# Dummy products in TensorE's waits, and feed-forward weights that meet both parts of the tokens in 512 columns

## The reference

```python
# first block, for i in 0, 1
h = x * (1 + sc_m) + sh_m
y = conformer_conv(h, ...) if i == 0 else short_gated_conv(h, ...)
x = layer_norm(ALPHA * x + (1 + g_m) * y, ...)
h = x * (1 + sc_f) + sh_f
y = hierarchical_moe(h, ...)                 # router, 32 experts, 2 of them per token
x = layer_norm(ALPHA * x + (1 + g_f) * y, ...)

# second block, for l in 0, 1
x = layer_norm_2(DN_ALPHA * x + 0.5 * swiglu(x, ffn1_in[l], ffn1_out[l]), ...)
x = layer_norm_2(DN_ALPHA * x + hybrid_mixer(x, ...), ...)
x = layer_norm_2(DN_ALPHA * x + 0.5 * swiglu(x, ffn2_in[l], ffn2_out[l]), ...)

def swiglu(x, w_in, w_out):                  # w_in 1024 x 5632, w_out 2816 x 1024
    gate, up = jnp.split(x @ w_in, 2, axis=-1)
    return (jax.nn.silu(gate) * up) @ w_out
```

## Time and profile before

| | |
|---|---|
| median of 3 runs | 2619.37 us (2616.03 to 2624.01) |
| profiled execution, its own time | 2622.48 us |
| span in its trace | 2620.7 us |
| PE busy | 2448.5 us (93%) |
| PEld busy | 1816.9 us (69%) |
| DVE busy | 1279.0 us (49%) |
| ACT busy | 886.8 us (34%) |
| POOL busy | 304.6 us (12%) |
| mean granted TensorE clock | 0.979 of full |

### The profile page before, as it was taken

How to read it: one execution, slowest core, us unless ns; L and a number is a source line. 1 busy time by engine, 2 the same in 40 slices (tenths; PEclk the granted TensorE clock), 3 DMA queues, 4 the chain that set the end, 5 groups by cost and what they waited for, 6 DMA issues and landing times.

```text
span 2620.7 us, 39277 instructions
## 1 busy us (share of the span) xinstructions
PE 2448.5 (93%) x16044; PEld 1816.9 (69%) x16045; DVE 1279.0 (49%) x2232; ACT 886.8 (34%) x1528; POOL 304.6 (12%) x371
## 2 busy tenths in 40 slices
PE   7999988998898998998899999999999999999998
PEld 4664434443685433343499899889989989988997
DVE  6573323222665332322354586665455458666545
ACT  2341111111332211111144465454444446545443
POOL 0210100000000010000000123330010012333001
PEclk8989999999998999999899999999999999999999
DMA  9987999999783999999937453343743745334371
GB/s 395 370 336 316 420 419 420 419 420 420 273 335 129 419 419 419 419 420 420 390 131 256 158 179 133 128 156 130 256 161 122 264 158 177 127 137 155 129 257 49
DMA packets 246345, 710.56 MB, mean 271 GB/s; under 512 B 11795, under 2 KB 165139, under 8 KB 189587
## 3 DMA queue, kind: packets, MB, share of 16 engines
q1 hardware_dynamic: 243810, 704.94, 70.5%
q10 hardware_dynamic: 2352, 3.06, 0.3%
HBM read 705.46 MB, written 1.05 MB: 270 GB/s over the span
## 4 chain that ended last, share of the span: by engine, by line
PE 72%; DMA 16%; DVE 6%; issue 2%; ACT 2%; POOL 1%; SPq 0%; DVEq 0%; ACTq 0%; POOLq 0%
PE w L899 19%; DMA ring<-in_e_w_up_dram 15%; PE w L1161 11%; PE y L939 11%; PE w L901 9%; PE w L1180 5%; PE w L1420 2%; PE y L1213 2%; PE y L806 1%; PE w L1405 1%; PE w L1135 1%; PE y L1369 1%; PE w L1001 1%; DVE wsp L1525 1%; DMA ring<-in_ada_w_dram 1%
## 5 line engine op out<-in xcount | busy, mean ns | idle before, releaser
L1525 DVE TENSOR_TENSOR wsp<-ring,wsp 128x1024 fp32r<-128x1024 f32 (+1 forms) x464 | 573.1, 1241 | 387.1 <-ACT wsp L1515 386.7
L899 PE MATMUL w<-hh,wsp 128*128 128x256 f32 x4672 | 613.4, 284 | 5.7 <-DVE wsp L1525 4.1
L899 PEld LDWEIGHTS w<-hh,wsp 128*128 128x128 f32 x4672 | 584.7, 191 | 28.5 <-issue 17.3
L1515 ACT CAST wsp<-ring 128x1024 fp32r<-128x1024 f32 (+1 forms) x464 | 482.1, 1045 | 354.4 <-PE w L901 171.9
L1161 PE MATMUL w<-ring,arena 128*64 128x512 f32 x2016 | 459.3, 600 | 77.2 <-DMA ring<-in_e_w_up_dram 72.5
L1161 PEld LDWEIGHTS w<-ring,arena 128*64 128x64 f32 x2016 | 153.8, 137 | 344.2 <-issue 342.3
L901 PE MATMUL w<-hl,wsp 128*128 128x256 f32 x2336 | 327.7, 283 | 0.0
L901 PEld LDWEIGHTS w<-hl,wsp 128*128 128x128 f32 x2336 | 301.3, 192 | 0.0
L939 PE MATMUL y<-wsp,zsp 128*128 128x512 f32 x1104 | 266.8, 391 | 2.9 <-POOL zsp L2747 2.6
L2011 DVE TENSOR_TENSOR ht<-w,ht 128x256 f32<-128x256 f32 x64 | 39.5, 618 | 440.9 <-ACT ht L2543 440.9
L2543 ACT ACTIVATE ht<-w 128x256 f32<-128x256 f32 x64 | 40.0, 626 | 625.3 <-PE w L1161 625.3
(11 more groups left out here) (334 smaller groups left out, 2478.7 us busy)
## 6 DMA issues: line engine op xcount, KB each, us to landing
ring<-in_e_w_gate_dram SPq DMA_DIRECT2D x126, 1024.0 KB, 13.6
ring<-in_e_w_up_dram SPq DMA_DIRECT2D x126, 1024.0 KB, 15.8
ring<-in_e_w_down_dram SPq DMA_DIRECT2D x124, 1024.0 KB, 13.6
ring<-in_ffn_in_dram SPq DMA_DIRECT2D x88, 1024.0 KB, 6.1
ring<-in_ada_w_dram SPq DMA_DIRECT2D x48, 1024.0 KB, 14.6
ring<-in_w_in_dram SPq DMA_DIRECT2D x48, 1024.0 KB, 5.0
ring<-in_ffn_out_dram SPq DMA_DIRECT2D x44, 1024.0 KB, 6.3
ring<-in_b_w_in_dram SPq DMA_DIRECT2D x12, 1024.0 KB, 11.8
```

Source lines behind the costliest of these rows:

```text
L899: pe.matmul(dst, a[:, kc * m:(kc + 1) * m], hh[:, kc, :], start=kc == 0 and j == 0, stop=False)
L1515: ac.copy(shaped(halves(i)[0], u.shape), u.cut(ring[:, u.piece % NSLOT, :])).then_inc(*mark("w_high", i))
L1525: ve.tensor_tensor(shaped(lo, u.shape), u.cut(ring[:, u.piece % NSLOT, :]), shaped(hi, u.shape).bitcast(F32), ALU.subtract).then_inc(*mark ...
```

## The change

Two things are changed. First, a helper `keep_busy(bank, times)` issues float32 products of the identity with 256 columns of `vecs` into a PSUM bank whose content nobody reads. It is called ahead of some waits of TensorE: 4 times in each router before the second token part; 7 times (3 in layer 0) before and after the ranks; 7 times before the last `combine` of each layer; 5 times before part 0 of the norms `ffn0` and `ffn1`; 6 times before part 1 of the norms `n00`, `n01`, `n02`, `n10`, `n11`.

Second, in the feed-forwards the tiles `hh` and `hl` become halves of one tile `hx`. Each high weight piece now meets both at once in one matmul of 512 columns, which puts the two partial sums side by side into a whole bank; the low weight piece adds to the first half. Gate and up therefore take a bank each, and VectorE adds the halves of each with a `tensor_reduce`, the gate into `hid` and the up into `upb`. Silu and the multiplication then read these.

```diff
+            def keep_busy(bank, times):
+                for _ in range(times):
+                    pe.matmul(bank[:, 0:T], ident, vecs[:, 0:T], start=True, stop=True)

             router(l, n):            # for t in range(2):
+                    if t:
+                        keep_busy(WB[2], 4)
             to_feature_later(n):     # for t in range(2):
+                    if n[0:3] == "ffn" and t == 0:
+                        keep_busy(WB[3], 5)
+                    elif n[0] == "n" and t == 1:
+                        keep_busy(WB[0], 6)
                     pe.wait_ge(*at("diag", n, t))
             moe(l, n):
+                keep_busy(WB[0], 7 if l else 3)
                 pe.wait_ge(*at("route_v", l, "oo", 1))
...
+                keep_busy(WB[0], 7 if l else 3)
             combine(p):
+                    pe.wait_ge(*at("ct", l, p))
+                    if p == E // 2 - 1:
+                        keep_busy(WB[moe_banks(l).index(("turn", E - 1)) % 4], 7)
                     pe.wait_ge(*at("ye", "low", l, p))

+            def proj_wide(dst, i):
+                wh, wl = halves(i)
+                pe.wait_ge(*low_done(i))
+                for kc in range(KC):
+                    if kc == KC - 1:
+                        pe.matmul(dst[:, 0:T], wl[:, kc * P:(kc + 1) * P], hh[:, kc, :], start=False, stop=False)
+                    ins = pe.matmul(dst[:, :], wh[:, kc * P:(kc + 1) * P], hx[:, :, kc, :], start=kc == 0, stop=kc == KC - 1)
+                    if kc < KC - 1:
+                        pe.matmul(dst[:, 0:T], wl[:, kc * P:(kc + 1) * P], hh[:, kc, :], start=False, stop=False)
+                ins.then_inc(*mark("w_used", i))

             # TensorE, ffn
-                    b = WB[k % 4]
+                    gate_b, up_b = ffn_banks(k)      # (WB[0], WB[3]) or (WB[1], WB[2])
                     if k == 0:
-                        first_two([b[:, 0:T], WB[3][:, T:2 * T]], i, n)
+                        first_wide([gate_b, up_b], i, n)     # the same 48 matmuls of 256 columns
                     else:
-                        if k >= 3:
-                            pe.wait_ge(*at("hid", key, max(k - 4, 0)))
-                        proj(b[:, 0:T], i)
-                        proj(b[:, T:2 * T], i + 1)
+                        if k >= 2:
+                            pe.wait_ge(*at("up_sum", key, k - 2))
+                        proj_wide(gate_b, i)
+                        proj_wide(up_b, i + 1)

             # VectorE, ffn
+                    weight_lows(ve, i + (2 if k == 0 else 3))
+                    ve.wait_ge(*at("w_used", i))
+                    if k >= 4:
+                        ve.wait_ge(*at("z_lo", key, k - 4))
+                    ve.tensor_reduce(hid[:, k % 4, :], gate_b[:, :].rearrange("p (a t) -> p t a", a=2), AX, ALU.add)
                     weight_lows(ve, i + 4)
+                    ve.wait_ge(*at("w_used", i + 1))
+                    ve.tensor_reduce(upb[:, k % 2, :], up_b[:, :].rearrange("p (a t) -> p t a", a=2), AX, ALU.add)
                     ve.wait_ge(*at("silu_f", key, k))
-                    ve.tensor_tensor(hid[:, k % 4, :], WB[k % 4 if k else 3][:, T:2 * T], hid[:, k % 4, :], ALU.mult)
+                    ve.tensor_tensor(hid[:, k % 4, :], upb[:, k % 2, :], hid[:, k % 4, :], ALU.mult)

             # ScalarE, ffn
-                    ac.wait_ge(*at("w_used", i + 1))
-                    ac.activation(hid[:, k % 4, :], WB[k % 4][:, 0:T], ACT.Silu)
+                    ac.wait_ge(*at("gate_sum", key, k))
+                    ac.activation(hid[:, k % 4, :], hid[:, k % 4, :], ACT.Silu)
```

More of the change, by code:

```diff
@@ L304, in program @@
         vv = sb("vv", [P, 2, D])
-        hh = sb("hh", [P, KC, T], F32R)
-        hl = sb("hl", [P, KC, T], F32R)
+        hx = sb("hx", [P, 2, KC, T], F32R)
+        hh, hl = hx[:, 0, :, :], hx[:, 1, :, :]
         ht = sb("ht", [P, 4, 2, T])
@@ L367, in program @@
         hid = area(0, 4, T)
+        upb = ht[:, 1, :, :]
         vh = zsp[:, :, :, :].rearrange("p a b t -> p (a b t)").rearrange("p (t d) -> p t d", t=2)
@@ L674, in bank_end, with ffn_banks @@
             return f | (1 if t and n != "ffn0" else 3)
+        def ffn_banks(k):
+            return (WB[1], WB[2]) if k % 2 else (WB[0], WB[3])
         def z_tiles(key, f):
@@ L933, in first_two, with first_wide @@
                     ins.then_inc(*mark("w_used", i + u))
+            def first_wide(dsts, i, n):
+                parts = [halves(i + u) for u in range(2)]
+                for u in range(2):
+                    pe.wait_ge(*at("w_high", i + u))
+                    for kc in range(KC):
+                        if u == 0:
+                            pe.wait_ge(*at("h_hi", n, 1, kc))
+                        pe.matmul(dsts[u][:, 0:T], parts[u][0][:, kc * P:(kc + 1) * P], hh[:, kc, :], start=kc == 0, stop=False)
+                for u in range(2):
+                    pe.wait_ge(*low_done(i + u))
+                    for kc in range(KC):
+                        pe.matmul(dsts[u][:, 0:T], parts[u][1][:, kc * P:(kc + 1) * P], hh[:, kc, :], start=False, stop=kc == KC - 1)
+                for u in range(2):
+                    for kc in range(KC):
+                        if u == 0:
+                            pe.wait_ge(*at("h_lo", n, kc, 1))
+                        ins = pe.matmul(dsts[u][:, T:2 * T], parts[u][0][:, kc * P:(kc + 1) * P], hl[:, kc, :], start=kc == 0, stop=kc == KC - 1)
+                    ins.then_inc(*mark("w_used", i + u))
+            def proj_wide(dst, i):
+                wh, wl = halves(i)
+                pe.wait_ge(*low_done(i))
+                for kc in range(KC):
+                    if kc == KC - 1:
[4 more added lines that the diff above has]
+                ins.then_inc(*mark("w_used", i))
             def row_half(k, n, i, zh, zl, t, h):
@@ L1207, in combine @@
                     i = p % 2
+                    pe.wait_ge(*at("ct", l, p))
+                    if p == E // 2 - 1:
+                        keep_busy(WB[moe_banks(l).index(("turn", E - 1)) % 4], 7)
                     pe.wait_ge(*at("ye", "low", l, p))
-                    pe.wait_ge(*at("ct", l, p))
                     for t in range(2):
@@ L2127, in ffn @@
                 for k in range(22):
+                    gate_b, up_b = ffn_banks(k)
+                    weight_lows(ve, i + (2 if k == 0 else 3))
+                    ve.wait_ge(*at("w_used", i))
+                    if k >= 4:
+                        ve.wait_ge(*at("z_lo", key, k - 4))
+                    ve.tensor_reduce(hid[:, k % 4, :], gate_b[:, :].rearrange("p (a t) -> p t a", a=2), AX, ALU.add).then_inc(*mark("gate_sum", key, k))
                     weight_lows(ve, i + 4)
+                    ve.wait_ge(*at("w_used", i + 1))
+                    ve.tensor_reduce(upb[:, k % 2, :], up_b[:, :].rearrange("p (a t) -> p t a", a=2), AX, ALU.add).then_inc(*mark("up_sum", key, k))
+                    ve.wait_ge(*at("up_sum", key, k))
                     ve.wait_ge(*at("silu_f", key, k))
-                    ve.tensor_tensor(hid[:, k % 4, :], WB[k % 4 if k else 3][:, T:2 * T], hid[:, k % 4, :], ALU.mult).then_inc(
+                    ve.tensor_tensor(hid[:, k % 4, :], upb[:, k % 2, :], hid[:, k % 4, :], ALU.mult).then_inc(
                         *mark("hid", key, k))
@@ L2586, in ffn @@
                     weight_highs(ac, i + 4)
-                    if k >= 4:
-                        ac.wait_ge(*at("z_lo", key, k - 4))
-                    ac.wait_ge(*at("w_used", i + 1))
-                    ac.activation(hid[:, k % 4, :], WB[k % 4][:, 0:T], ACT.Silu).then_inc(*mark("silu_f", key, k))
+                    ac.wait_ge(*at("gate_sum", key, k))
+                    ac.activation(hid[:, k % 4, :], hid[:, k % 4, :], ACT.Silu).then_inc(*mark("silu_f", key, k))
                     if k >= 4:
```

## The result

The changed kernel takes 2607.29 us (median of 7 runs, 2604.74 to 2608.85). The kernel before took 2619.37 in the same session (7 runs, 2614.44 to 2625.24). The ratio is 0.995, 95% interval 0.9939 to 0.9961, so it is faster by 12.1 us. The forecast was 20.2 us less, at 2599: right in direction, inside the ends that its terms gave (2592 to 2613), and too large by two thirds. The span in the trace went from 2620.7 to 2605.5, 15.2 us less, and the mean granted clock from 0.979 to 0.991.

What follows compares the result with a forecast made beforehand. TensorE was taken to bound the feed-forwards; -14.5 + 5.4 + 1.2 - 8.0 - 4.5 - 1.7 + 1.9 = -20.2 us gave 2599 us against the median, range 2592 to 2613.

Steps and rivals of the forecast that it cites:

- wide products: Feed-forward projections: merging 8 pairs of matmuls saves 0.086 us in each of 168 projections, 14.5 us off TensorE.
- start of each feed-forward: Block 1's gate product starts some 1.4 us late, as VectorE's subtraction stands behind the reduce of gate 0; +5.4 us.
- ends: End of each feed-forward: a reduce and a subtraction now precede the last z; 0.3 us each, +1.2 in all.
- norms: Norms n00 to n11: six dummies fit TensorE's 3.08 us idle before part 1 and keep the clock up; -8.0 us.
- last combinings: Last combinings and their norms: dummies fit in the waits and the work behind runs at full clock; -4.5 us.
- router, layer 1: Layer 1's router: dummies fill the waits, so ranks and gathering come at full clock; -1.7 us (-3.4 to +1).
- router, layer 0: Layer 0's router: no wait before part 1, so four dummies delay the turn by 1.86 us; +1.9 in sum.
- rival 3: Feed-forwards: VectorE becomes the bound from a reduce of about 2.0 us; about 2645 us at 2.5; chance 0.03.
- rival 2: Norms, combinings, layer 1's router: dummies do not hold the clock, their 14.2 us go; about 2616 us; chance 0.09.
- Rival 4: Projections: a 256-column matmul's extra 13 ns belongs mostly to its columns; merging gains a quarter; about 2610 us; chance 0.03.

Runs made afterwards that it cites:

- experiment 3: The changed kernel with VectorE's subtraction for weight unit 2 back ahead of the reduce of gate 0; 2597.89 us, 0.9914 of the kernel before.
- experiment 1: The kernel before with all the change's dummy products and its own narrow projections; 2609.2 us, 0.9955 of the kernel before.
- Experiment 7: The changed kernel with each projection's eight 512-column products together and the eight 256-column ones after them; 2597.5 us, 0.9914 of the kernel before.
- experiment 4: The changed kernel with the loads of the next norm's gain and bias five weight pieces later in SyncE's queue; 2604.36 us, 0.994 of the kernel before.
- experiment 2: The changed kernel with every dummy product left out, so the wide products alone; 2614.5 us, 0.9969 of the kernel before.
- experiment 6: The changed kernel with two dummy products instead of six before part 1 of norms n00 to n11; 2603.64 us, 0.9937 of the kernel before.
- experiment 10: The kernel before with four dummy products added ahead of block 5 of the first feed-forward; 2622.45 us, 1.0005 of the kernel before.

## Why the prediction was right, and where its size failed

By its own steps, from the two traces (us):

| step | forecast | measured | from |
|---|---|---|---|
| wide products | -14.5 | -11.7 | 84 pairs of projections x (5.63 - 5.75) = -10.1; rows 2.73 instead of 2.75, -1.6 |
| start of each feed-forward | +5.4 | +5.7 | 1.24 in each, 0.96 of it idle, and 0.25 more in three of them from the faster norms |
| ends | +1.2 | -1.0 | last z: 0.43 of wait instead of 0.65 in each |
| block 8 | 0 | +2.5 | 0.50 to 0.77 in each |
| norms | -8.0 | -9.7 | 4.14 to 4.16 instead of 5.33 to 6.65 |
| last combinings | -4.5 | -4.9 | 2.0 and 2.9 |
| router, layer 1 | -1.7 | -3.2 | 28.43 to 25.19 |
| router, layer 0 | +1.9 | +2.4 | 23.97 to 26.41 |
| ahead of layer 0's router | 0 | +2.0 | untouched code; 6.8 us at half clock instead of 3.4 |
| hybrids | 0 | +2.4 | 255.61 to 256.46, 254.15 to 255.66 |
| the rest | 0 | +0.4 | expert loops and projections |
| sum | -20.2 | -15.1 | spans: -15.2 |

The steps that the change touched add up to -19.9 in the traces, next to the forecast's -20.2. That is luck in part: the wide products (2.8) and block 8 (2.5) came out worse than forecast, the ends (2.2), norms (1.7) and layer 1's router (1.5) better. The first hybrid's loss, shown below, is not in this sum. The router's gain is the least sure: eight other traces with its dummies have 24.98 to 26.84 us there, where this one has 25.19.

**What held.** TensorE is the bound of the feed-forward, and a matmul saved there is time saved. The reduces took 0.69 us and VectorE did not become the bound (rival 3). The wait at the start has the place and the cause given (experiment 3), and nearly the size: 1.24 us each, 1.35 was forecast. The dummies hold the clock where they fill a wait that is there anyway (experiment 1, and all 40 norms with six of them), against rival 2, and cost time in layer 0's router, where there was none.

**The wide products were sized too high.** The step took 8 x 0.229 + 8 x 0.120 for a projection, from rows in which matmuls of one width follow one another. None showed what alternating widths cost. Alternating, a projection is 2.815 instead of 2.79, so a pair gains 0.12 and not 0.17. Experiment 7 shows that the alternation takes the rest. Why a wide matmul behind a narrow one takes 0.235 is open; the reason given in that experiment's expectation, the time that the next weights have to load, was not tested. Rival 4 is out: grouped, 16 merged pairs gain 5.75 - 5.56 = 0.19 us, 12 ns each, nearly all of the 13 that a 256-column matmul holds above its columns. By the rule in the Trainium skill ("TensorE: Matmul & The Clock Gate", "Back-to-back issue gap") each would gain 2.5 ns; no run here bears that out.

**A queue was left out.** The prediction went through VectorE's, ScalarE's and TensorE's order in a block and gave the low part of the next unit 1.3 us over. It did not look at SyncE, whose queue waits for VectorE's use of `lnp`, with weights behind it. 2.5 us; experiment 4 shows it. Of the steps missed, this is the one that the trace of before could have shown: both the late issues and what stood behind them were in it (nothing issued from 1326.28 to 1359.38).

**The clock's gain is smaller in the medians than in the trace.** The norms were priced on five falls of the clock in one execution. Experiments 2, 6 and 10 show norms at full clock with none or two dummies, so some of those falls may be missing in another execution of the same kernel. The profiled execution of before was also 3.1 us above its median, while that of after was at its median; this is what separates the traces' -15.2 from the medians' -12.1. The mean granted clock of each run shows it over more executions: 0.977 to 0.985 in 34 runs of the kernel before on the three chips, and its time goes with it (on the third chip the four runs at 0.984 and 0.985 took 2612.46 to 2617.94 us, the others, at 0.978 to 0.981, 2618.59 to 2626.75). With the dummies it was 0.988 to 0.994 in all 45 runs of nine kernels. So the dummies do raise the clock every time, but by how much depends on the execution of before that is taken; mine was at 0.979. Which norm falls how often in the executions without a trace is not known.

The 2.0 us ahead of the router and the 1.5 in the second hybrid, where nothing was changed, are of the same kind: half-clock stretches that lie elsewhere in each trace. One is at 2307.8 to 2311.2, inside the second hybrid, which takes 254.2 us in the two traces without such a stretch and 255.4 to 255.9 in the ten with one. The 0.85 in the first hybrid is not: both traces have one such stretch there. With one, traces with wide products have 256.3 to 256.5 us and those with narrow ones 255.6 to 255.7; without one it is 255.0 to 255.1 and 254.4. So the wide products' kernel pays 0.6 to 0.9 us there, a side effect that the forecast did not have. Its cause was not followed up.

## What to carry to other kernels

When matmuls are merged, price them at the rate in the very sequence that will be issued; alternating widths were slower than the same matmuls sorted by width (8.36 against 8.31 us a block), and sorting them cost nothing. When a step gets shorter, go through every queue that feeds it, the DMA issues with their waits included, because what had slack may have none now. A fall of the clock behind one wait in one profile is not a fixed cost of that wait: filling waits with dummies did pay here, but only where TensorE waited anyway; in layer 0's router, where it did not, they cost time. And when several edits each seem to gain more than their places in the trace show, look at what moved in the places that nobody touched.

## What the runs showed of the hardware

- A 512-column fp32r matmul in a stream of its kind takes 0.227 us, alternating with 256-column ones 0.235 (narrow ones 0.117 there, 0.120 among themselves). Eight and eight are 2.78 grouped and 2.815 alternating.
- A reduce of pairs of float32 that lie 1 KB apart in PSUM takes 0.69 us for 256 results, the same as a plain read of 512.
- The granted clock fell to the 1.2 GHz level after waits of about 3.1 us in some traces and stayed at 2.4 GHz after the same waits in others (4.15 us against 5.3 to 6.6 for the same work), ten falls behind 15 such waits in three traces. With six dummies in the wait there was none behind 40 in eight traces, with two dummies one behind five. What decides in the first case is not known.
- In layer 0's router of the changed kernel the clock fell during the dummies themselves, at 177.9 us: there four dummies took 3.06 us instead of 1.86.
- A queue whose next transfer waits holds back those behind it: SyncE issued nothing for 32 us ahead of two small loads, and with these five weight pieces later the wait of 0.50 to 0.77 us on TensorE in block 8 was gone in all four feed-forwards.
